# Norms of a 1024-wide diffusion backbone step: two half weight panels around the lone norm, first token block by itself, and an earlier root and broadcast in the late norms

## The reference

```python
def rms_norm(x, g):
    y = x32 * lax.rsqrt(jnp.mean(x32 * x32, axis=-1, keepdims=True) + EPS)
    return y.astype(x.dtype) * g

def modulate(x, g, shift, scale):
    return rms_norm(x, g) * (1.0 + scale) + shift

x = x + m[2] * (0.5 * swiglu(modulate(x, norm_g[0], m[0], m[1]), w_in[0], w_out[0]))
out, aux = mixer(modulate(x, norm_g[1], m[3], m[4]))
x = x + m[5] * out
x = x + m[8] * (0.5 * swiglu(modulate(x, norm_g[2], m[6], m[7]), w_in[1], w_out[1]))
```

## Time and profile before

| What | Value |
|---|---|
| Median of 3 runs (lowest, highest) | 1610.54 us (1607.89, 1610.88) |
| Profiled execution, its own time | 1608.08 us |
| Its span, first to last instruction | 1605.8 us |
| PE busy | 1552.3 us (97%) |
| DVE busy | 1102.3 us (69%) |
| ACT busy | 646.3 us (40%) |
| POOL busy | 34.1 us (2%) |
| Mean granted clock of TensorE | 0.994 |

### The profile page before, as it was taken

How to read it: one execution, slowest core, us unless ns; L and a number is a source line. 1 busy time by engine, 2 the same in 40 slices (tenths; PEclk the granted TensorE clock), 3 DMA queues, 4 the chain that set the end, 5 groups by cost and what they waited for, 6 DMA issues and landing times. The chain is left out here.

```text
span 1605.8 us, 21909 instructions
## 1 busy us (share of the span) xinstructions
PE 1552.3 (97%) x8893; PEld 1463.9 (91%) x8893; DVE 1102.3 (69%) x1782; ACT 646.3 (40%) x962; POOL 34.1 (2%) x37
## 2 busy tenths in 40 slices
PE   9999999999879999999999999999887999999999
PEld 6999999878659999999999999997775799999998
DVE  5878787778586788776678878765676867443332
ACT  4433332343385633333353333223345756333221
POOL 0000000000020000000000000000200000000000
PEclk9999999999999999999999999999899999999999
DMA  9755566433204365545626555541230023333333
GB/s 393 257 223 212 217 219 220 143 138 125 105 1 157 119 223 219 217 179 179 216 106 236 218 202 220 218 164 60 77 121 27 2 89 122 130 111 127 117 127 111
DMA packets 50707, 254.72 MB, mean 159 GB/s; under 512 B 6320, under 2 KB 8496, under 8 KB 34864
## 3 DMA queue, kind: packets, MB, share of 16 engines
q1 hardware_dynamic: 48032, 250.11, 42.9%
q10 hardware_dynamic: 2576, 3.22, 0.6%
HBM read 250.54 MB, written 2.77 MB: 158 GB/s over the span
## 5 line engine op out<-in xcount | busy, mean ns | idle before, releaser
L966 DVE TENSOR_TENSOR w_lo<-w_raw,w_hi 128x2048 fp32r<-128x2048 f32 (+2 forms) x186 | 375.8, 2021 | 228.0 <-ACT w_hi L578 227.0
L1588 PE MATMUL ps<-hx_hi,w_hi 128*128 128x384 f32 (+1 forms) x1472 | 498.6, 339 | 2.9 <-DVE w_lo L966 2.2
L1589 PE MATMUL ps<-hx_lo,w_hi 128*128 128x384 f32 (+1 forms) x1472 | 496.8, 337 | 0.0
L1590 PE MATMUL ps<-hx_hi,w_lo 128*128 128x384 f32 (+1 forms) x1472 | 496.6, 337 | 0.0
L578 ACT ACTIVATE w_hi<-w_raw 128x2048 fp32r<-128x2048 f32 (+2 forms) x186 | 316.1, 1700 | 423.0 <-DMA w_raw<-in_w_out 217.2
L1588 PEld LDWEIGHTS ps<-hx_hi,w_hi 128*128 128x128 f32 x1472 | 277.1, 188 | 6.8 <-DVE w_lo L966 3.2
L1589 PEld LDWEIGHTS ps<-hx_lo,w_hi 128*128 128x128 f32 x1472 | 276.7, 188 | 0.0
L1590 PEld LDWEIGHTS ps<-hx_hi,w_lo 128*128 128x128 f32 x1472 | 276.4, 188 | 0.0
L1590 PE MATMUL ps<-g_hi,w_lo 128*128 128x384 f32 x704 | 235.2, 334 | 0.0
L1588 PE MATMUL ps<-g_hi,w_hi 128*128 128x384 f32 x704 | 235.2, 334 | 0.0
L1589 PE MATMUL ps<-g_lo,w_hi 128*128 128x384 f32 x704 | 235.1, 334 | 0.0
(11 more groups left out here) (234 smaller groups left out, 1392.0 us busy)
## 6 DMA issues: line engine op xcount, KB each, us to landing
w_raw<-in_w_in SPq DMA_DIRECT2D x88, 1024.0 KB, 4.8
wm<-in_w_mod SPq DMA_DIRECT2D x128, 512.0 KB, 5.7
w_raw<-in_w_out SPq DMA_DIRECT2D x64, 704.0 KB, 4.1
w_raw<-in_w_qkv SPq DMA_DIRECT2D x12, 1024.0 KB, 4.7
wm_first<-in_w_mod_first SPq DMA_DIRECT2D x8, 1024.0 KB, 19.5
w_raw<-in_w_o SPq DMA_DIRECT2D x8, 1024.0 KB, 4.7
w_raw<-in_w_qup SPq DMA_DIRECT2D x8, 576.0 KB, 3.7
w_raw<-in_w_down SPq DMA_DIRECT2D x4, 1024.0 KB, 4.7
```

What stands on the lines that cost most here:

```text
L966: nc.vector.tensor_tensor(w_lo[:, slot, 0:width], w_raw[:, slot, 0:width], w_hi[:, slot, 0:width].bitcast(F32), ALU.subtract).then_inc(w_l ...
L1588: nc.tensor.matmul(out, l_hi, r_hi, start=first, stop=False)
L1589: nc.tensor.matmul(out, l_hi, r_lo, start=False, stop=False)
L1590: return nc.tensor.matmul(out, l_lo, r_hi, start=False, stop=last)
```

## The change

In norms 1 and 4 the second weight panel of the next projection is converted in two halves of 1024 columns: the first while the last x tile of ffn_out is being made, the second on ACT right behind the last square, on DVE at k=3. The third panel moves to k=5 (ACT) and k=7 (DVE). The sum of squares is taken in two parts: three products of `sqacc` ahead of the wait for the last square, three behind it, one bank (4, 5, 6) for each block. The broadcast of block 0 comes first, alone, into bank 3, and is repeated with the others into bank 6; DVE works block by block; PE waits for high and low parts of a block apart. Fillers are 3, 2 and 2 instead of 6, 2 and 5, into bank 2. In the late norms the root is ACT's and the reciprocal DVE's instead of DVE's mean and POOL's power, the broadcast stands after k=3 instead of k=5, and Sqrt and Silu of the small tile `var` bring tables in at set places.

```diff
@@ gpsimd @@
-            norm(0)
+            pool.wait_ge(var_ready, 1)
+            nc.gpsimd.tensor_tensor(rstd[:], var[:], nhalf[:, 0:NB], ALU.pow).then_inc(rstd_ready, 1)
...
-            norm(2)
-            norm(3)
...
-            norm(5)
@@ scalar @@
+            def high_half(n, i, half):
+                slot = n % SLOTS
+                act.wait_ge(w_loaded[slot], 16 * (n // SLOTS + 1))
+                act.wait_ge(panel_used, n - SLOTS + 1)
+                cols = slice(HALF * half, HALF * half + HALF)
+                nc.scalar.activation(w_hi[:, slot, cols], w_raw[:, slot, cols], ACT.Copy).then_inc(
+                    w_hi_done if half else half_hi, 1)
+            def root(n):
+                act.wait_ge(ss_ready, n + 1)
+                ss = ps[:, 4:4 + NB, T] if n in PLAIN else ps[:, 6, T:T + NB]
+                nc.scalar.activation(std[:], ss, ACT.Sqrt, bias=epsc[:, 0:1],
+                                     scale=1.0 / D).then_inc(std_ready, 1)
@@ scalar, norm @@
-                act.wait_ge(ss_ready, n + 1)
-                nc.scalar.activation(std[:], ps[:, 6, T:T + NB], ACT.Sqrt, bias=epsc[:, 0:1],
-                                     scale=1.0 / D).then_inc(std_ready, 1)
+                root(n)
...
-                    if k == 1:
-                        high_of(*norms[n], 1)
-                    if k == 4:
+                    if k == 5:
                         high_of(*norms[n], 2)
@@ scalar, late_norm @@
+                root(n)
                 high(base + 2)
+                nc.scalar.activation(var[:], var[:], ACT.Silu)
                 act.wait_ge(bc_ready, n + 1)
@@ scalar, ffn_out and wo @@
-                if f in (0, 2):
-                    act.wait_ge(dve_consts, 1)
-                    nc.scalar.activation(std[:, 0:1], epsc[:, 0:1], ACT.Sqrt)
+                if f < 3:
+                    nc.scalar.activation(var[:], var[:], ACT.Sqrt)
...
+                    if j == 2 * KD - 1 and f in (0, 2):
+                        high_half(base + j + 2, f // 2, 0)
...
+                elif f < 3:
+                    high_half(base + 2 * KD + 1, f // 2, 1)
...
+                nc.scalar.activation(var[:], var[:], ACT.Sqrt)
@@ vector @@
+            def reciprocal(n):
+                v.wait_ge(std_ready, n)
+                nc.vector.reciprocal(rstd[:], std[:]).then_inc(root_ready, 1)
...
+                reciprocal(n)
+                block_scaled(0)
+                block_full(0)
+                block_scaled(1)
+                block_scaled(2)
+                block_low(0)
+                block_full(1)
+                block_low(1)
+                block_full(2)
+                block_low(2)
...
-                    if k == 2:
-                        low_of(*norms[n], 1)
-                    if k == 5:
+                    if k == 3:
+                        low_half(PHASE[norms[n]][0] + 1, i, 1)
+                    if k == 7:
                         low_of(*norms[n], 2)
@@ vector, ffn_out and wo @@
-                    invert(late)
+                    reciprocal(late)
                     low(base + 2 * KD + 1)
+                elif after:
+                    low_half(base + 2 * KD + 1, f // 2, 0)
@@ tensor @@
+                if n in PLAIN:
+                    pe.wait_ge(x_squared, KD * (n + 1))
+                    for b in range(NB):
+                        mm = nc.tensor.matmul(ps[:, 4 + b, T:T + 1], square[:, b * P:(b + 1) * P], ones[:, 0:1],
                                               start=False, stop=True)
                 mm.then_inc(ss_ready, 1)
...
                 if n in PLAIN:
-                    pe.wait_ge(root_ready, PLAIN[n] + 1)
...
+                    nc.tensor.matmul(ps[:, 3, 0:P], rstd[:, 0:1].to_broadcast([P, P]), ident[:], start=True,
+                                     stop=True).then_inc(bc_first, 1)
...
-                fill(6)
+                fill(3)
                 sum_squares(n)
                 fill(2)
                 broadcast(n)
-                fill(5)
+                fill(2)
...
-                        elif k == 5:
+                        elif k == 3:
                             broadcast(n)
@@ tensor, project @@
+                            pe.wait_ge(blk_hi, at)
+                            nc.tensor.matmul(out, h_hi[:, k, cols], hi, start=True, stop=False)
+                            nc.tensor.matmul(out, h_hi[:, k, cols], lo, start=False, stop=False)
+                            pe.wait_ge(blk_lo, at)
+                            mm = nc.tensor.matmul(out, h_lo[:, k, cols], hi, start=False, stop=False)
```

More of the change, by code:

```diff
@@ L460, in lat_val @@
             return KD * n + k + 1 - sum(1 for p in PLAIN if p <= n)
-        def roots(n):
-            return n + 1 - sum(1 for p in PLAIN if p <= n)
         def adds(n, k):
@@ L970, in low_of, with low_half @@
                 low(PHASE[name, i][0] + k)
+            def low_half(n, i, half):
+                slot = n % SLOTS
+                cols = slice(HALF * half, HALF * half + HALF)
+                if half:
+                    v.wait_ge(w_hi_done, n + 1)
+                else:
+                    v.wait_ge(half_hi, i + 1)
+                ins = nc.vector.tensor_tensor(w_lo[:, slot, cols], w_raw[:, slot, cols],
+                                              w_hi[:, slot, cols].bitcast(F32), ALU.subtract)
+                if half:
+                    ins.then_inc(w_lo_done, 1)
             def mod_half(q, s, panel, loaded, before):
@@ L1096, in norm @@
                 i = PLAIN[n]
-                blocks = [(b, slice(b * P, (b + 1) * P), 1 if b < 2 else 0) for b in range(NB)]
-                v.wait_ge(std_ready, i + 1)
-                nc.vector.reciprocal(rstd[:], std[:]).then_inc(root_ready, 1)
-                v.wait_ge(bc_ready, n + 1)
-                for b, blk, c in blocks:
-                    nc.vector.tensor_tensor(temp(n, 0)[:, blk], x[:, 0, blk], ps[:, 6, blk],
-                                            ALU.mult).then_inc(blk_tmp, 1)
@@ L1104, in norm, with rows, block_scaled @@
-                for b, blk, c in blocks:
+                def rows(b):
+                    return slice(b * P, (b + 1) * P)
+                def block_scaled(b):
+                    if b == 0:
+                        v.wait_ge(bc_first, i + 1)
+                    else:
+                        v.wait_ge(bc_ready, n + 1)
+                    src = ps[:, 3, 0:P] if b == 0 else ps[:, 6, rows(b)]
+                    nc.vector.tensor_tensor(temp(n, 0)[:, rows(b)], x[:, 0, rows(b)], src, ALU.mult).then_inc(blk_tmp, 1)
@@ L1620, in fill @@
                 for _ in range(count):
-                    nc.tensor.matmul(ps[:, 4, 0:P], ident[:], ones[:], start=True, stop=True)
+                    nc.tensor.matmul(ps[:, 2, 0:P], ident[:], ones[:], start=True, stop=True)
             def norm(n):
-                fill(6)
+                fill(3)
                 sum_squares(n)
```

48 lines of the change are left out of this document (28 added, 20 removed).

## The result

| What | Before | After |
|---|---|---|
| Median (lowest, highest) of the runs made together | 1608.33 us (1607.37, 1611.39), 7 runs | 1598.02 us (1595.65, 1602.78), 7 runs |
| Profiled execution, its own time | 1608.08 us | 1597.20 us |
| Its span | 1605.8 us | 1595.6 us |
| Mean granted clock | 0.994 | 0.993 |

The ratio of after to before is 0.9934, 95% interval 0.9918 to 0.9950. The forecast was 1601.5, from a gain of 9.0.

A forecast was written before the change was run, and what follows sets the result against it. PE was taken as busy nearly all the time, so only its holes and fillers could give time back. 8.0 us (norms 1 and 4) plus 1.0 (late norms) made 9.0, from 1610.54 to 1601.5; range 1598 to 1606.

The forecast's parts named there:

- (e): Norms 1 and 4, projection tiles 2 to 7: waits of 2.31 us at tile 2 and 1.03 at tile 5 vanish.
- (a): Norms 1 and 4, split sum of squares: sum ready 0.66 us earlier, ACT's root at 308.99 instead of 309.65.
- (b): Norms 1 and 4: half panels take ACT 1.06 and DVE 1.25 us, hidden, ACT's second with 0.1 us spare.
- (c): Norms 1 and 4, first block alone: first product at about 311.05 instead of 312.95, 1.9 us earlier.
- (d): Norms 1 and 4, tile 1: starts 0.72 us earlier, with a 1.65 us stall behind DVE's block work.
- Rival C: Norms 1 and 4: the halves are not hidden and delay root and tiles; gain only 5.6 us, 1604.9; chance 0.11.
- Late norms: Norms 2, 3, 5: copy 0.45 us earlier shortens PE's waits in 2 and 5, nothing in 3; 1.0 us altogether.
- Rival A: Norms 2, 3, 5 give nothing, the copy being held by something unseen; gain 8.0 us, 1602.5; chance 0.08.
- rival B: A table switch holds ACT 2.6 us; waits in norms 2 and 5 grow 0.9 each; 1604.3; chance 0.04.
- Rival D: After norm 1 or 4 an unmoved stage gives back one norm's 4.0 us or both; 1605.5 to 1609.5; chance 0.08.
- Rival E: Norms 1 and 4: PE's clock falls to 1.2 GHz for both projections; 24.6 us slower, 1635; chance 0.05.

The follow-up runs named there:

- early_tile1: Changed kernel with tiles 0 and 1 taking high-part products first and DVE scaling tile 1 between tile 0's blocks, lone norms only; median 1598.07 us, ratio 0.9935.
- late_old: Changed kernel with norms 2, 3 and 5 as before the change (POOL's power, DVE's mean, broadcast after k=5, no dummy activations); median 1599.79 us, ratio 0.9932.
- table_three: Changed kernel with two more table switches, Sqrt and Silu, behind the dummy Silu of the late norms; one run, 1607.36 us.
- no_fill: Changed kernel with all fillers of the lone norms taken out; median 1602.51 us, ratio 0.9963.
- no_silu: Changed kernel without the dummy Silu activation ahead of the late norms' copy; median 1596.61 us, ratio 0.9932.
- panels_only: Changed kernel keeping the half panels, but with blocks together, one sum of squares and fillers 6, 2 and 5; median 1599.67 us, ratio 0.9934.
- whole_panels: Changed kernel keeping the first block by itself, but with two whole panels at the old places on ACT and DVE; median 1606.23 us, ratio 0.9969.

## Why the prediction came out as it did

Direction and mechanism were right, the size was not: the forecast was 3.5 us too high, and 1598.0 lies 1.0 us below the forecast's own range of 1599 to 1604. That it still lies inside the wide range of 1598 to 1606, by 0.02 us, is luck. Two terms were mis-sized, the base and the sum.

2.2 of the 3.5 us are the **base**. I took the three-run median of 1610.54; with four more runs the same kernel's median was 1608.33. The profiled execution's own 1608.08, which gave 1599.1 in my sum, came nearer, but nothing told me so: beside the experiments the kernel before had medians of 1612.55, 1608.59, 1608.87 and 1608.59. A base of three runs was the weakest term, and I gave it no width of its own.

The other 1.3 is the **sum**, 9.0 against 10.3: 0.48 too little in the lone norms, which is step (e) below; 0.47 too little in the late norms as profiled; and 0.34 from places that were not in the sum at all.

(a) Root: forecast 2.5 us behind the fillers' start, measured 2.42 (306.44 to 308.86). Right.
(b) Halves: forecast 1.06 and 1.25 us, measured 1.06 (1.04) and 1.21; hidden, with none of the 0.1 spare. Rival C did not happen in norm 4 in any profile.
(c) First product: forecast 4.55, measured 4.43.
(d) Tile 1: forecast 1.65 of stall, measured 1.68 (8.29 - 4.43 - 2.18). Right, and it was next in line as named: early_tile1 removed it, and tiles 3 and 7 came next.
(e) Tiles 2 and 5: no waits, as forecast. This is the step that failed in size: I took the waits off, not the 0.11 us that PE needs to get going behind each, 0.22 per norm. With (c) that makes 4.0 into 4.3; measured 4.20 and 4.28. Term: 8.0 forecast, 8.48 measured.

**Late norms**: 1.0 forecast, 1.20 by late_old (1.47 between the two profiles, of which 0.28 in norm 3 is an ACT delay that only the profile of before has). The 0.45 for norms 2 and 5 was 0.55 and 0.47 in this profile, and 0.45 and 0.39 on average over ten. Norm 3, which I put at nothing because its buffers are shared, gave 0.18 every time. That the total of 1.0 agrees with the average is partly luck: of my 1.0, 0.1 stood for a wait on POOL and nothing for norm 3. The three added Sqrt loads were covered, as forecast: product by product, PE loses nothing in the stages behind them. Rival A is refuted by late_old, rival B by table_three: a switch costs its load and its activation, 1.5 us.

**Not in the sum at all**: 0.26 from transposes in attention, 0.58 from the clock, 0.50 given back where a panel's load took 0.5 us longer. The last two are of the kind that changes from one execution to the next; they net to almost nothing here. Rival D did not happen: PE's lead of 8.5 us from the norms is still there at the end.

**Rival E**, the clock, I weighed wrongly in kind. I expected all or nothing: two projections at half rate, 24.6 us. The changed kernel as profiled has the clock full in both lone norms, but no_fill shows the danger to be real and small: in norm 4, 6.8 us at 1.2 GHz, with a first product 0.4 us later, cost 1.05 us in all; in norm 1 the stretch was 2.7 longer, of which 1.3 is the late panel. With fillers the clock falls in norm 1 where PE had stood 0.8 us or more for the last square (five profiles; it stayed full in a sixth, no_silu), not behind the wait at tile 1, which is 1.5 us in the undisturbed profiles too. That wait for the square is what my step had not seen: I treated norms 1 and 4 as one pattern, and in the single profile of before they were.

**Open**: what decides where the other half-clock stretches fall. They lie near 24, in attention (430 to 475) and in mla (1118 to 1230 us), in places that change with the execution; all stretches together are 14 to 38 us of a span. I made no experiment on them. Open too is why the clock stayed full in norm 1 of no_silu after a wait of 0.80 us, where it fell in panels_only after the same wait, and why a panel's load takes longer in some executions.

## What to carry to other kernels

When a wait is removed, name the next thing in the same engine's order and price it: here 2.0 us at the first product were worth 0.7 at tile 1, 1.2 at tile 1 were worth 0.6 at the end, and 0.6 from the high parts alone were worth nothing. Put work that waits for a transfer, and everything queued behind it, where nothing on the path follows it: two products behind a panel's subtraction made the norm hang on when the panel landed. A table preload pays only if the engine is idle; on a busy ScalarE ahead of the copy that everyone waits for, it costs its full 1.4 us there and saves it where nobody looks.

## What the runs showed of the hardware

- A wait costs PE something beyond its idle time: in both kernels the next product starts 0.34 us after the one that waited for a tile's low part, instead of 0.23, and 0.31 us after the first product of the projection.
- A table switch is 1.28 us of load and 0.20 of activation, 1.51 from one to the next, with nothing behind it (three in a row in table_three).
- Without fillers the granted clock fell for 6.8 us in both lone norms. With them it fell only in norm 1, in five of the six profiles in which PE had stood 0.80 us or more for the last square, and never in norm 4, where it stood 0.16 or less.
- The load of one 1 MB panel, issued 11.25 us before the end of ffn_out in every profile, took 4.6 to 6.4 us to land (before 4.62, whole_panels 6.39).
